# A two-layer sequence model block on one core: input in pieces, a residual taken tile by tile, a deeper last attention head, and low parts of a norm on GpSimd

## The reference, cut to what matters

```python
def block(x, ctx, ...):                        # x: 512 tokens of 1024 features, ctx: 256 tokens
    h = rms_norm(x, norm_pre_mix)              # input norm
    x = x + rms_norm(hybrid_mixer(h), norm_post_mix)      # recurrent heads + gated convolution
    h = rms_norm(x, norm_pre_ffn)
    x = x + rms_norm(conv_ffn(h), norm_post_ffn)          # second residual
    # then two layers of attention over x and ctx, each: modulate, mix, gate, project, residual, layer norm
    for mixer in (mla_mixer, diff_mixer):
        shift, scale, gate = split(silu(c) @ ada_w + ada_b)
        h, h_c = x * (1 + scale) + shift, ctx * (1 + scale_c) + shift_c
        o = mixer(h, h_c) @ out_w
        x = layer_norm(ALPHA * x + gate * o)
        # ctx the same after the first layer
    return x
# diff_mixer: 8 heads. p = softmax(q1 k1) - lambda * softmax(q2 k2); o = p v;
# each head's o is rms-normed (g_sub) and multiplied by silu(gate)
```

## Time and profile before

| | |
|---|---|
| median of 3 runs | 1648.27 us (1647.25 to 1651.25) |
| profiled execution | 1646.52 us |
| its span, first to last instruction | 1644.7 us |
| mean granted TensorE clock | 0.989 |
| busy: PE, PE weight load, DVE, ACT, POOL | 95%, 77%, 61%, 42%, 56% |

### The profile page before, as it was taken

How to read it: one execution, slowest core, us unless ns; L and a number is a source line. 1 busy time by engine, 2 the same in 40 slices (tenths; PEclk the granted TensorE clock), 3 DMA queues, 4 the chain that set the end, 5 groups by cost and what they waited for, 6 DMA issues and landing times.

```text
span 1644.7 us, 27170 instructions
## 1 busy us (share of the span) xinstructions
PE 1569.4 (95%) x11032; PEld 1271.0 (77%) x11032; DVE 995.1 (61%) x1296; ACT 696.5 (42%) x1210; POOL 917.5 (56%) x732
## 2 busy tenths in 40 slices
PE   6999888999999999989999999999999999999887
PEld 5677887678888888868877777768878888888775
DVE  5699786747556540053455756664776666566666
ACT  4653775333222220032246565662264434444662
POOL 5354787929999999964470312336634444433152
PEclk9999999999999999999999999999999999999998
DMA  5221104422222243241120000004321110111211
GB/s 197 77 79 75 55 4 158 154 103 77 102 102 96 84 158 123 104 164 52 52 73 5 26 1 26 0 1 154 125 94 51 52 52 28 50 52 52 103 52 52
DMA packets 18876, 126.07 MB, mean 77 GB/s; under 512 B 2096, under 2 KB 2352, under 8 KB 4304
## 3 DMA queue, kind: packets, MB, share of 16 engines
q1 hardware_dynamic: 18624, 124.02, 20.8%
q10 hardware_dynamic: 144, 0.52, 0.1%
HBM read 122.43 MB, written 2.10 MB: 76 GB/s over the span
## 4 chain that ended last, share of the span: by engine, by line
PE 55%; issue 19%; POOL 12%; DVE 9%; ACT 4%; DMA 1%; POOLq 0%; ACTq 0%; SPq 0%; DVEq 0%
POOL w_hi L687 8%; PE banks L1358 5%; PE banks L1538 4%; PE banks L1541 4%; PE banks L1539 4%; POOL w_lo L678 4%; PE banks L1337 4%; PE banks L1220 3%; PE banks L1225 3%; PE banks L1221 3%; PE banks L1593 2%; PE banks L816 2%; PE banks L817 2%; PE banks L818 2%; PE banks L1573 2%
## 5 line engine op out<-in xcount | busy, mean ns | idle before, releaser
L687 POOL TENSOR_TENSOR w_hi<-raw,der 128x512 fp32r<-128x512 f32 x296 | 333.9, 1139 | 416.2 <-PE banks L1541 178.6
L678 POOL TENSOR_TENSOR w_lo<-raw,w_hi 128x512 fp32r<-128x512 f32 x336 | 476.2, 1431 | 61.8 <-ACT w_hi L1682 61.5
L816 PE MATMUL banks<-h_hi,w_hi 128*128 128x512 f32 x464 | 184.2, 397 | 0.3 <-DVEq L2372 0.3
L817 PE MATMUL banks<-h_lo,w_hi 128*128 128x512 f32 x464 | 180.7, 389 | 0.0
L818 PE MATMUL banks<-h_hi,w_lo 128*128 128x512 f32 x464 | 180.6, 389 | 0.0
L1538 PE MATMUL banks<-h_hi,w_hi 128*128 128x512 f32 (+1 forms) x384 | 145.6, 379 | 0.1
L1539 PE MATMUL banks<-h_lo,w_hi 128*128 128x512 f32 (+1 forms) x384 | 130.6, 355 | 0.0
L2207 ACT ACTIVATE dP<-banks,der 128x768 f32<-128x768 f32 x64 | 57.8, 903 | 158.8 <-DVE der L3046 158.8
L1541 PE MATMUL banks<-h_hi,w_lo 128*128 128x512 f32 (+1 forms) x384 | 115.9, 356 | 0.0
L740 POOL TENSOR_TENSOR Of<-Of,Ls 128x768 f32<-128x768 f32 x8 | 14.7, 1831 | 173.2 <-DVE Ls L2843 173.2
L816 PEld LDWEIGHTS banks<-h_hi,w_hi 128*128 128x128 f32 x464 | 87.1, 188 | 25.8 <-issue 7.5
(11 more groups left out here) (534 smaller groups left out, 3825.8 us busy)
## 6 DMA issues: line engine op xcount, KB each, us to landing
raw<-in_stream SPq DMA_DIRECT2D x84, 1024.0 KB, 4.8
ada_home<-in_ada_w SPq DMA_DIRECT2D x18, 1024.0 KB, 7.3
raw<-in_ada_w SPq DMA_DIRECT2D x4, 1024.0 KB, 4.8
xT<-in_x_t SPq DMA_DIRECT2D x2, 1024.0 KB, 7.0
xT<-in_x_t SPq DMA_DIRECT2D x1, 2048.0 KB, 7.2
ada_end<-in_ada_w SPq DMA_DIRECT2D x2, 1024.0 KB, 6.2
out_t<-z SPq DMA_DIRECT2D x8, 256.0 KB, 2.1
ctxT<-in_ctx_t SPq DMA_DIRECT2D x1, 1024.0 KB, 7.0
```

The source lines that it names most:

```text
L678: return pool.tensor_tensor(lo[:, h, part(i), :], raw_tiles(half)[:, part(i), :], hi[:, h, part(i), :], ALU.subtract)
L687: pool.tensor_tensor(hi[:, h, part(i), :], raw_tiles(half)[:, part(i), :], one, ALU.mult).then_inc(hi_done, 1)
L816: pe.matmul(banks[b][:, :], hi, tile(rhs_hi, k), start=(at_k == 0), stop=False)
L817: pe.matmul(banks[b][:, :], hi, tile(rhs_lo, k), start=False, stop=False)
```

## The change: what it does

Four parts, in the order of time.

1. x is loaded in four pieces of two tiles and block 0 in a quarter, a quarter and a half, all issued without a wait between them; block 1 goes out when the second piece has landed. PE runs ten 128 x 128 products on constants (`WARM`) as soon as these are there. ACT takes the tiles as they come, with most squares at the end. GpSimd holds the third quarter of block 0 back until DVE has made all 8 low parts.
2. In the second residual each tile is scaled and added at once, and GpSimd holds the split of the second `mla_in` block back until three low parts are made.
3. In the middle norm, centring and multiplication alternate, the gains come before the root's spread is awaited, GpSimd makes the low parts of tiles 0, 1, 2, 4 and 6, DVE those of 3, 5 and 7.
4. The last head has a second pair of weight buffers (`dP_last`), so that weighing goes one query tile ahead of mixing; root and table load come first; ACT scales heads 0 to 3, GpSimd heads 4 to 6. The late `ada_w` blocks get homes of their own in the space of `h2_hi` and `h2_lo` and are loaded at the end of the last head's projections, so that the first two blocks of the last projection come through the ordinary `weights` queue and are split early. The second late `ada_product` moves to the end of the head.

```diff
+    ada_late_home = reg("ada_late_home", [P, 2 * KT * 256], 67)
+    ada_end = reg("ada_end", [P, (107 - 83) * 256 + KT * 256], 83)
...
+    LOW_BY_POOL = (0, 1, 2, 4, 6)
+    dP_last = [reg(f"dP_last{i}", [P, TA], 97 + 3 * i) for i in range(2)]
+    def weighed(h, u):
+        return (dP_last if h == B_HEADS - 1 and u // 2 % 2 else dP)[u % 2]
+    def weighed_free(h, u):
+        return mixed.at(4 * h + (max(0, u // 2 - 1) if h == B_HEADS - 1 else u // 2))
... (SP)
+        first_weights(0, 1, s_quarter[0])
+        x_tiles(0)
+        x_tiles(1)
+        first_weights(1, 2, s_quarter[1])
+        x_tiles(2)
+        x_tiles(3)
+        first_weights(2, PARTS, raw_full[0])
-        weights(0, 1)
-        sp.wait_ge(s_x[0], 16)
-        sp.dma_start(xT[:, 4:8, :], x_t[:, 4:8, :]).then_inc(s_x[1], 16)
+        sp.wait_ge(s_x[1], 16)
         weights(1, 2)
...
-        sp.wait_ge(z_centred, KT)
-        for b in (18, 19):
-            sp.wait_ge(ada_full[b % 4], 16 * (b // 4))
+        for b, done in ((18, (z_gated, 4)), (19, (z_centred, KT))):
+            sp.wait_ge(*done)
+            sp.wait_ge(*ada_loaded(b - 4))
             ada_block(b)
-        weights(STREAM["diff"] + 2, STREAM["diff_out"])
+        weights(STREAM["diff"] + 2, STREAM["diff_out"] + 2)
+        sp.wait_ge(block_done, STREAM["diff_out"])
         for b in (20, 21):
-            sp.wait_ge(split_full, STREAM["diff_out"] + b - 21)
             ada_block(b, b - 4)
-        sp.wait_ge(block_done, STREAM["diff_out"])
         ada_block(22)
         ada_block(23)
-        for n in (STREAM["diff_out"], STREAM["diff_out"] + 1):
-            weights_behind(n, 20 + (n - STREAM["diff_out"]) % 2)
... (GpSimd)
+                if first:
+                    pool.wait_ge(s_quarter[i] if i < 2 else raw_full[half], 16)
+                    if i == 2:
+                        pool.wait_ge(h_ready, KT)
...
+        pool.wait_ge(mh_ready, 3)
+        with pool.Fori(0, (before - second) // 2) as i:
...
+        for k in LOW_BY_POOL:
+            pool.wait_ge(mh_hi, KT + k + 1)
+            pool.wait_ge(mh_ready, KT + k)
+            pool.tensor_tensor(h2_lo[:, k, :], zh[:, k % 2, :], h2_hi[:, k, :], ALU.subtract).then_inc(mh_ready, 1)
...
+        pool.wait_ge(*o_inverse.at(1))
+        for h in range(BY_ACT, B_HEADS - 1):
+            o = O_tok[:, :, P * h:P * h + P]
+            inverse = o_rs[:, 4 * h:4 * h + 4].unsqueeze(2).broadcast_to([P, 4, P])
+            pool.tensor_tensor(o, o, inverse, ALU.mult).then_inc(o_scaled_pool.sem, 1)
... (PE)
+        for _ in range(WARM):
+            pe.matmul(banks[5][:, 0:P], ones, ident, start=True, stop=True)
...
+        diff_scores(h, 2)
+        diff_scores(h, 3)
+        ada_product(ADA_LATE)
+        diff_turn(h, 0)
+        diff_scores(h, 4)
+        diff_values(h, 0)
+        diff_scores(h, 5)
+        diff_scores(h, 6)
+        diff_turn(h, 1)
+        diff_values(h, 1)
+        diff_scores(h, 7)
+        diff_turn(h, 2)
+        diff_values(h, 2)
+        pe.wait_ge(*p_full.at(8 * B_HEADS))
+        turn_o(0)
+        turn_o(1)
+        diff_turn(h, 3)
+        ada_product(ADA_LATE + 1)
         diff_values(h, 3)
... (ACT)
+        for i in range(4):
+            act.wait_ge(s_x[i], 16)
+            for k in (2 * i, 2 * i + 1):
                 input_high(k)
+            if i == 1:
+                input_square(0)
+            if i == 2:
+                input_square(1)
+        for k in range(2, KT):
+            input_square(k)
...
+        root(0, 4 * h)
         take_v(h)
+        act.activation(der[:, ROOT + 4:ROOT + 5], der[:, 127:128], ACT.Exp)
+        take_vt(h)
         weigh(h, 0)
         weigh(h, 1)
         act.wait_ge(*o_inverse.at(1))
         scale_heads(0, 1)
+        weigh(h, 2)
+        scale_heads(1, 2)
+        take_turn(h, 0)
+        weigh(h, 3)
+        weigh(h, 4)
+        scale_heads(2, 3)
+        take_turn(h, 1)
+        weigh(h, 5)
+        square(h, 0)
+        weigh(h, 6)
+        scale_heads(3, 4)
+        take_turn(h, 2)
+        weigh(h, 7)
... (DVE)
+        for k in range(2):
+            post_scaled(fout, "post_ffn", k)
+            chain.wait()
+            x_brought(k)
+        for k in range(2, KT):
+            post_scaled(fout, "post_ffn", k)
+            modulated_low(k - 2)
+            chain.wait()
+            x_brought(k)
...
         ada_columns(7)
         gains(0)
+        x_centre(4)
         dve.wait_ge(z_sum, 5)
         x_norm(0)
+        x_centre(5)
         x_norm(1)
+        x_centre(6)
+        x_norm(2)
         x_centre(7)
+        x_norm(3)
         ada_columns(8)
         ada_columns(9)
         gains(CT)
...
+        top(h, 0)
         dve.wait_ge(o_root, 1)
         dve.reciprocal(o_rs[:, 0:4 * h], o_rs[:, 0:4 * h]).then_inc(o_inverse.sem, 1)
+        top(h, 1)
+        top(h, 2)
+        mix(h, 0)
+        top(h, 3)
+        copy_turn(h, 0)
+        top(h, 4)
+        mix(h, 1)
+        out(h, 0)
+        ada_columns(ADA_LATE)
...
```

More of the change, by code:

```diff
@@ L224, in col @@
         return prm[:, bass.ds(i + PCOL[name], n)] if not isinstance(i, int) else prm[:, PCOL[name] + i:PCOL[name] + i + n]
-    s_x = [sem(f"x_loaded{k}") for k in range(2)]
+    s_x = [sem(f"x_loaded{k}") for k in range(4)]
     s_const = sem("constants_loaded")
@@ L729, in _ @@
         before = BLK1 + 2
-        first = out0 + 7
-        assert first % 2 == 0
-        with pool.Fori(0, (before - first) // 2) as i:
+        first, second = out0 + 7, STREAM["mla_in"] + 1
+        assert first % 2 == 0 and second % 2 == 0 and before % 2 == 0
+        with pool.Fori(0, (second - first) // 2) as i:
             for s in range(2):
                 split(2 * i + (first + s), s, i + first // 2)
-        assert (before - first) % 2 == 0
+        pool.wait_ge(mh_ready, 3)
+        with pool.Fori(0, (before - second) // 2) as i:
+            for s in range(2):
+                split(2 * i + (second + s), s, i + second // 2)
         def finish(p):
@@ L773, in _ @@
             split(n, 1, n // 2)
-        rest = n + n % 2
-        with pool.Fori(0, (N_BLOCKS - rest) // 2) as i:
+        modulated = STREAM["diff"] + 2
+        assert n % 2 == 0 and modulated % 2 == 0
+        with pool.Fori(0, (modulated - n) // 2) as i:
+            for s in range(2):
+                split(2 * i + (n + s), s, i + n // 2)
+        for k in LOW_BY_POOL:
+            pool.wait_ge(mh_hi, KT + k + 1)
+            pool.wait_ge(mh_ready, KT + k)
+            pool.tensor_tensor(h2_lo[:, k, :], zh[:, k % 2, :], h2_hi[:, k, :], ALU.subtract).then_inc(mh_ready, 1)
+        rest, third = modulated, STREAM["diff_out"] + 2
+        assert rest % 2 == 0 and third % 2 == 0 and N_BLOCKS % 2 == 0
+        with pool.Fori(0, (third - rest) // 2) as i:
             for s in range(2):
                 split(2 * i + (rest + s), s, i + rest // 2)
-        if N_BLOCKS % 2:
-            split(N_BLOCKS - 1, 0, N_BLOCKS // 2)
+        pool.wait_ge(*o_inverse.at(1))
[3 more added lines that the diff above has]
+            pool.tensor_tensor(o, o, inverse, ALU.mult).then_inc(o_scaled_pool.sem, 1)
+        with pool.Fori(0, (N_BLOCKS - third) // 2) as i:
+            for s in range(2):
+                split(2 * i + (third + s), s, i + third // 2)
     @block.tensor
@@ L3000, in _ @@
         x_norm(4)
-        h_low(2)
         x_norm(5)
@@ L3007, in _ @@
         dve.tensor_copy(silu_last[:, :, :], silu_pad)
-        for k in range(4, KT):
+        for k in (5, 7):
             h_low(k)
@@ L3115, in gated_low @@
             dve.tensor_tensor(h2_lo[:, k, 0:T], og[:, k % 2, :], h2_hi[:, k, 0:T], ALU.subtract).then_inc(og_ready, 1)
+        top(h, 0)
         dve.wait_ge(o_root, 1)
         dve.reciprocal(o_rs[:, 0:4 * h], o_rs[:, 0:4 * h]).then_inc(o_inverse.sem, 1)
-        dve.wait_ge(*o_inverse.at(1))
-        for qt in range(1, 4):
-            top(h, 2 * qt)
-            top(h, 2 * qt + 1)
-            copy_turn(h, qt - 1)
-            mix(h, qt)
-            out(h, qt - 1)
-            if qt == 1:
-                ada_columns(ADA_LATE)
+        top(h, 1)
[7 more added lines that the diff above has]
+        ada_columns(ADA_LATE)
+        top(h, 5)
+        copy_turn(h, 1)
+        top(h, 6)
+        mix(h, 2)
+        out(h, 1)
+        top(h, 7)
+        copy_turn(h, 2)
+        mix(h, 3)
+        out(h, 2)
         gated(0)
@@ L3143, in _ @@
         ins.then_inc(o_scaled, 1)
-        for k in range(4, B_HEADS):
+        gated_low(3)
+        dve.wait_ge(ada_late, 2)
+        for k in range(5, B_HEADS):
             gated(k)
```

97 lines of the change are left out of this document (36 added, 61 removed).

## The result

The changed kernel takes 1636.74 us (median of 4 runs, 1635.48 to 1638.43), the kernel before beside it 1649.07 us (4 runs, 1647.25 to 1651.25). The ratio is 0.993, with a 95% interval from 0.9917 to 0.9944. A second set of five runs gave 1637.68 us against 1647.11 us, ratio 0.9939 (0.9927 to 0.9952). The change makes the kernel faster by 9.4 to 12.3 us; 1634.5 us was predicted.

A forecast was written before the change was run, and what follows sets the result against it. PE, busy for 95% of the span, was taken as the bound, so only its waits could pay. The terms 5.3 + 0.6 + 1.1 + 6.1 = 13.1 us gave 1634.5 us, range 1627 to 1642.5.

The forecast's parts named there:

- the spread at 22 to 24: Input: sign that the forecast is right, the root's spread ending at 22 to 24 us; later than 25 meant wrong.
- the low parts of `mla_in`: Second residual, sign: first low part 5 us nearer to the addition, last at the old distance, subtractions 1.5 us or more.
- cost nothing: Input: the ten warming products take PE from 3.9 to 9 us, before the first low part, at no cost.
- DVE's time beside the split: Second residual: beside GpSimd's split, subtractions take 1.58 us on 512 columns and 1.9 on 768, against 0.96 alone.
- what decides is the last low part: Second residual: the last low part sets the column's end; it comes 0.9 us later, the column ends 0.6 sooner.
- is held at the last two: Middle norm before the change: PE, with 1.7 us of work per tile, waits at the last two; 1.1 us gain forecast.
- does not move: Middle norm: PE's start stays, as the `ada_product` before it waits for a block landing 13.2 us after its issue.
- The 0.7 us that ACT was to lose at tile 4: Middle norm: DVE must wait for the `ada_product` ending just before 1199.73, so ACT loses 0.7 us.
- the half clock at the first late product: Last head: first `ada_product` at 1550.5 us, at half clock until 1553.9 as before; 7.5 us gain without it, 6.1 forecast.
- (a): Rival, 17%: engines meet less; second residual gives 5.3 us, input 6.7, with the rest 19.2: 1628 us.
- (b): Rival, 24%: half clock in last head, late block 1, DVE held in second residual; gain only 5.4 us, 1642.
- (c): Rival, 4%: queue serves all transfers alike, so late `ada_w` blocks and input pieces land late; slower, 1653 to 1655 us.

## Why the prediction was right

The time, 1636.74, is 2.2 us from the 1634.5 given, and the gain by stages is 14.3 us for a forecast 13.1. That the sum is so near is luck in part: two of the four parts came out 1.3 to 1.5 us above their term, one as much below, and 4 us were lost where the prediction had no term. The stages of parts 1 and 4 were forecast for the right reason, those of parts 2 and 3 were not. Of its signs, the spread at 22 to 24, the low parts of `mla_in` and the absent waits for late `ada_w` blocks came. Two did not: the sums of squares ended at 19.8 (17 to 19 given), and PE's first product of the last projection came 10.5 us sooner (12 to 14 given), for the 3.4 us lost in the recurrent part. Each step:

- Part 1, 5.3 forecast, 4.9 measured. The mechanism was right, down to ACT's high parts of block 1 ahead of the root. Two sizes cancel, which is luck: ACT's high parts ended a microsecond later than in the sum, the squares at 18.1 instead of 17.3, and the sums at 19.8 instead of 17.9; but block 1 landed at 16.9 (7.1 us after its issue, not 9.4) where 18.0 to 19.5 was given, so that ACT was through with it at 19.9, as the sum had it (20). The 1.5 us from the last bytes to the landing are an estimate that no row shows; the last piece landed at 13.2 for 12.7 forecast. The warming products "cost nothing" is near right: they bring some 0.6 us at the spread and cost up to 0.7 near 177 us.
- Part 2, 0.6 forecast, 1.9 measured. The low parts came as the sum had them, with a slower split and contention on each tile; in the scale of the kernel before they end at 731.3, 734.7, 738.1, 741.5 and 743.5, for 731.7 to 745.3 forecast. The term that was mis-sized is DVE's time beside the split: 1.39 and 1.52 us, not 1.9 and 1.6; only the last two low parts took 2.0. The sentence "what decides is the last low part" failed: with the old order the last low part is 2.2 us sooner and the column 1.6 us later, and with the same last low part (24.6 and 24.7 us into the stage) the column ended at 33.2 or 30.7. What decides as well is how much PE has left by then, after its wait for the first tile and the half clock behind it. The prediction had 1.05 us per tile at 2.4 GHz and no term for that.
- Part 3, 1.1 forecast, -0.15 measured. The step that failed is a reading of the kernel before, that PE "is held at the last two" tiles. Behind its first product it waits for a low part once there, 0.14 us, and its 16.0 us of work run from 10.2 us after the spread's start to 26.2. It was already bound by its own start, so with a start that "does not move" there was nothing to gain. That the start would not move was right as far as the load goes (the block lands at 6.4 us before, 6.6 and 6.4 in the changed kernel's two traces). Where the half clock leaves the start at 8.9 instead, PE waits 1.1 us for low parts, since tile 4's multiplication stands behind two takings of ada columns that GpSimd's low parts stretch to 0.68 and 1.65 us, and tile 6's low part takes 1.84 us on GpSimd; the stretch ends at 26.3 all the same. With both taken away it ended at 24.7. The 0.7 us that ACT was to lose at tile 4 was 1.25.
- Part 4, 6.1 forecast, 7.6 measured. The mechanism was right: weighing no longer waits for mixing, the second pair alone is worth 3.3 to 4.85. The term that failed is the half clock at the first late product, "as before": it was 1.0 throughout, and the last weighing came some 2 us sooner than in the sum. Two other traces of the same head have 6.8 us at 0.5 there and are 1.5 us longer; measured by them the part gives 6.1, the forecast itself. A cost of 0.7 us in the last stores, if it belongs to this part, had no term. The late `ada_w` blocks never made PE wait.
- The sum: 14.3 us in the stages, less 3.4 us in the recurrent part, which varies from execution to execution and may in part belong to the change, and 0.7 at the end.

Of the rivals, (a), 5.3 us in the second residual, is what the kernel has when the split is held back for all eight low parts: 33.41 - 27.51 = 5.9 us. (b) and (c) did not happen. The version with that wait is faster than both kernels, 1632.27 us. That wait together with tile 6 on DVE was not run.

## What to carry to other kernels

Where two engines hold each other up and one of them has time, hold it back until the other is through, not until it has begun: the wait for three of eight tiles was 0.8 us worse than none, the wait for all eight 3.2 us better. A long wait of PE can be dearer than it looks: after waits of 2.3, 3.4 and 6.8 us in the second residual the clock was at 0.5 for 3.4, 6.8 and 4.2 us of work, and with six waits of at most 1.1 us it stayed at 1.0. Judge an edit of a microsecond by the distance between fixed instructions, but in more than one trace, with the granted clock of each stretch beside it: stages that no edit touched moved by 1 to 1.6 us with the place of the half clock, and one trace alone showed a gain of 1.2 us in a start that the second trace of the same kernel did not have. Before a step is credited with a gain, look whether the engine waits there at all.

## What the runs showed of the hardware

- A DVE instruction of 0.17 us took 1.65 us beside a GpSimd instruction of 1.87 us and ended with it: small instructions lose the most.
- An addition that took 5.56 us in the kernel before took 1.70 us in the same order and beside the same split in another kernel. The long one was seen once; its cause stays open.
- A stop of PE of 0.2 to 0.8 us near 177 us, without a releaser, stands in all eleven traces of kernels with ten or twenty warming products at the start, and in none of the three without them. The cause stays open.
- PE's stops without a releaser in a stretch of small products, 0.5 to 4.5 us in all, differ between executions of one kernel (2.5 and 4.0 us), and with the clock that falls behind them make up 8 us of spread.
- The last head, with the same instructions, had 1.0 throughout in seven traces and 0.5 for 6.8 us in two others, which cost 1.5 us; in one it had 0.5 for 3.4 us, which cost 0.1.
- Where PE waits for a block, a half clock before the wait is hidden by it and one behind it is not: the first product came 8.7 to 9.1 or 10.2 to 10.3 us after the spread, the block landing at 6.3 to 6.6 in every trace.
